# Two of the last weight loads of a mixture-of-experts layer, cut differently

## The chip, the cores and the metric

The kernel runs on one core of a Trainium2 chip. Its time is device time in microseconds (us), the median of three runs. The engines are TensorE (PE, with its weight loads as PEld), VectorE (DVE), ScalarE (ACT), GpSimd (POOL) and SyncE (SP). Nearly all loads from HBM are issued by SP; each transfer is carried by the core's 16 DMA engines, and each of them works through its own queue in the order in which the transfers were issued. A load has landed when the last of its DMA engines has reported.

## The reference

One decoder layer in float32 on 256 tokens of width 1024: attention and convolution branches, then 32 experts of which each token uses four, then a gated output with a layer norm. Cut to the part that matters here:

```python
for e in range(N_EXPERTS):                              # 32 experts
    gu = t @ w_gate_up[e] + b_gate_up[e]                # (1024 x 2048)
    g, u = gu[:, :D_EXPERT], gu[:, D_EXPERT:]
    g = jnp.minimum(g, SWIGLU_LIMIT); u = jnp.clip(u, -SWIGLU_LIMIT, SWIGLU_LIMIT)
    act = (u + 1) * (g * jax.nn.sigmoid(SWIGLU_ALPHA * g))
    y = act @ w_down[e] + b_down[e]                     # (1024 x 1024)
    out = out + combine[:, e:e + 1] * y
...
ple = jax.nn.sigmoid(h @ w_ple_gate) * (p @ w_ple_proj)
x = layer_norm(h + ple, ln2_g, ln2_b)
```

## The kernel before

The front of the layer takes the first 230 us. Then the experts run one after the other. For each, TensorE gathers the tokens that chose it, multiplies them with the gate and up weights, turns the sums, multiplies with the down weights and adds the rows to the output. An expert's weights are 12 MB in six pieces of 2 MB, c = 0 to 5: four of gate and up, two of down. Each piece is a tile of 128 partitions by 4096 floats (16 KB in a partition, `PAIR`) and feeds 16 records of matmuls of 128x512 (L488).

SP loads the pieces in the order in which TensorE uses them. They go into a ring of 11 places in SBUF (`slot_no`, `place_of`), and before each load SP waits until TensorE has read what lay there (`pair_read(last_in[n])`: `chunk_used`, `gu_done` or `d_done`). Pieces are numbered by `load_no(e, c)`. For the experts 5 to 29 two neighbouring pieces are joined to one transfer of 4 MB where their places lie side by side (the list `JOINED`); it waits for both places and raises one semaphore, for which both pieces wait on TensorE (`arrival`). Experts 30 and 31 are loaded in single pieces, and the last pieces of expert 31 in parts: piece 2 in its two rows (L401), piece 3 as its gate halves (L394) and then its two up halves (L396), piece 5 in two parts (L406). Behind them come two pieces of 2 MB of the gate of the output (L732, `w_pg`) and the two layer norm vectors (L735, L736). TensorE uses `w_pg` at L1398, in 128 records; the first 16 of these need the first piece alone.

Each semaphore `e_in[slot]` counts 16 for each transfer (`counts`), and TensorE waits in `pair(n)` for the count in `arrival[n]`. If an expert has more than 64 tokens it takes another branch with two rounds; in the run below the experts 29 to 31 take one round.

Of the kernel before, what the change touches and what calls it, by code (L numbers as in the profile page):

```python
# [7 lines left out]
D, S, P = 1024, 256, 128  # L8
# [9 lines left out]
NE, TOPE = 32, 4  # L18
# [24 lines left out]
PAIR = 2 * SLOT  # L43
# [39 lines left out]
def program(nc, x, xT, pT, w_in, consts1, consts2, b_in, w_oa, w_oc, w_out,  # L83
# [4 lines left out]
    with ctx:  # L88
# [3 lines left out]
        def sem(name):  # L92
            return ctx.enter_context(nc.semaphore(name))
# [5 lines left out]
        def view(at, n):  # L99
            return arena[:, at:at + n]  # L100
# [127 lines left out]
        e_in = [sem(f"expert_slot{i}_in") for i in range(ES)]  # L228
# [117 lines left out]
        PIECES = {6: 2, 10: 2, **{ES + i: 2 for i in range(CPE)}}  # L346
        slots, slot_no, last_in = list(range(ES)), [], []
# [7 lines left out]
        def place_of(n):  # L355

            return ((NF - NS + 1) // 2 % (NS // 2) + slot_no[n]) % ES

        def slot_of(n, size=PAIR):

            return view(RING + PAIR * place_of(n), size)

        def load_no(e, c):
            return e * CPE + c + (1 if e >= PP_E else 0)

        JOINED = [load_no(e, c) for e in range(5, NE - 2) for c in (0, 2, 4)]
        JOINED = [n for n in JOINED if place_of(n + 1) == place_of(n) + 1]
        counts, arrival = [0] * ES, []
        for n in range(NMP + CPE):
            if n == SPARE:  # L370
                arrival.append(None)
            elif n - 1 in JOINED:
                arrival.append(arrival[n - 1])
            else:
                counts[slot_no[n]] += 16 * PIECES.get(n, 1)
                arrival.append((slot_no[n], counts[slot_no[n]]))

        def rows_of_two(e, c):
            if c < 4:
                return w_gu[bass.ds(e, 1), c // 2 * 512:(c // 2 + 1) * 512, :].rearrange("e (p r) d -> p (e r d)", r=4)  # L380
            return w_dn[bass.ds(e, 1), :, :].rearrange("e p d -> p (e d)")

        def pair_source(e, c):
            return rows_of_two(e, c)[:, c % 2 * PAIR:(c % 2 + 1) * PAIR]

        def load_pair(sp, n, e, c, piece=None):
            if n == SPARE:
                for to, at in ((spare_row, slice(SLOT, PAIR)), (slot_of(n)[:, 0:SLOT], slice(0, SLOT))):
                    sp.dma_start(to, pair_source(e, c)[:, at]).then_inc(own_row_in, 16)
                return  # L390
            if n == LAST:
                to = slot_of(n).rearrange("p (r d) -> p r d", r=2)
                of = pair_source(e, c).rearrange("p (r d) -> p r d", r=2)
                sp.dma_start(to[:, :, 0:1024], of[:, :, 0:1024]).then_inc(e_in[slot_no[n]], 16)  # L394
                for r in range(2):
                    sp.dma_start(to[:, r, 1024:2048], of[:, r, 1024:2048]).then_inc(last_up_in[r], 16)  # L396
                return
            if n == LAST - 1:
                for row, done in enumerate((e_in[slot_no[n]], own_row_in)):
                    at = slice(row * SLOT, (row + 1) * SLOT)  # L400
                    sp.dma_start(slot_of(n)[:, at], pair_source(e, c)[:, at]).then_inc(done, 16)  # L401
                return
            if n == NG - 1:
                for half, done in enumerate((e_in[slot_no[n]], last_down_in)):
                    at = slice(half * SLOT, (half + 1) * SLOT)
                    sp.dma_start(slot_of(n)[:, at], pair_source(e, c)[:, at]).then_inc(done, 16)  # L406
                return
            if piece is not None:
                size = PAIR // PIECES[n]
                at = slice(piece * size, (piece + 1) * size)  # L410
                sp.dma_start(slot_of(n)[:, at], pair_source(e, c)[:, at]).then_inc(e_in[slot_no[n]], 16)
                return
            if n in JOINED:
                sp.dma_start(slot_of(n, 2 * PAIR), rows_of_two(e, c)).then_inc(e_in[slot_no[n]], 16)
                return
            sp.dma_start(slot_of(n), pair_source(e, c)).then_inc(e_in[slot_no[n]], 16)

        def pair_read(n):
            e, c = divmod(n - (1 if n > PP else 0), CPE)
            if c == 3:  # L420
                return gu_done, 2 * e + 2
            if c == CPE - 1:
                return d_done, 3 * e + 2
            return chunk_used, e * (CPE - 2) + (c + 1 if c < 4 else c)
# [228 lines left out]
        with nc.Block() as block:  # L653
            @block.sync
            def _(sp):
# [8 lines left out]
                def early(n, piece=None):  # L664
                    load_pair(sp, n, n // CPE, n % CPE, piece)
# [46 lines left out]
                for n in range(ES, NG):  # L712
                    if n in PIECES:
                        for i in range(PIECES[n] - 1):
                            sp.wait_ge(piece_used, pieces.up())
                            load_pair(sp, n, *divmod(n, CPE), i)
                        if n == ES + SPARE:
                            continue
                        sp.wait_ge(*pair_read(last_in[n]))
                        load_pair(sp, n, *divmod(n, CPE), PIECES[n] - 1)  # L720
                        continue
                    if n == PP or n - 1 in JOINED:
                        continue
                    sp.wait_ge(*pair_read(last_in[n]))
                    if n in JOINED:
                        sp.wait_ge(*pair_read(last_in[n + 1]))
                    load_pair(sp, n, *divmod(n - (1 if n > PP else 0), CPE))
# [1442 lines left out]
```

## Time and profile before

| | us |
|---|---|
| median of 3 runs | 1165.41 (1165.16 to 1165.5) |
| the profiled execution, its own time | 1165.17 |
| its span in the trace | 1163.3 |
| TensorE busy | 1134.7 (98% of the span) |
| 16 DMA engines, first queue (SP's loads) | 90.0% of 16 engines' span, 439.79 MB |

Read the busy shares with care: a TensorE that waits 2 us here and 1 us there for weights still counts as 98% busy. What a change to a late load is worth is read from the last wait for a DMA, and from how much later than its need each following load lands.

### The profile page before, as it was taken

To read this page: it belongs to the slowest core of one execution; us is meant where nothing else is said; L and a number is where in the kernel's file an instruction comes from. 1 tells how busy PE (TensorE), PEld (TensorE's weight loads), DVE (VectorE), ACT (ScalarE), POOL (GpSimd) and SP (SyncE) were. 2 spreads that over 40 slices of the span, in tenths; PEclk is the share of its full clock that TensorE was granted. 3 is DMA by queue.
4 is the path that set the end of the run, shared out by engine and by line. 5 is a ranking of instruction groups with operands and counts; after the bars stand their busy time and mean duration, and the time that the engine had idled before them with its cause. 6 is when DMAs were issued, how large, how long until landed. Compare 5 with 4: busy or idle time off the path is not lost.

```text
span 1163.3 us, 13812 instructions
## 1 busy us (share of the span) xinstructions
PE 1134.7 (98%) x5632; PEld 578.2 (50%) x5632; DVE 302.1 (26%) x790; ACT 182.5 (16%) x391; POOL 11.5 (1%) x26
## 2 busy tenths in 40 slices
PE   9999999999999999999999999999999999999997
PEld 7888888734344443434343344443434343433346
DVE  0549943411113122111111212121111111111126
ACT  1214220212121211111011011111111111101012
POOL 0020000000000000000000000000000000000000
PEclk9999999999999999999999999999999999999999
DMA  9975357699999999999999999999999999999981
GB/s 360 384 280 217 137 234 317 265 361 426 428 427 424 436 431 431 427 431 431 430 427 431 429 412 436 431 432 429 432 431 432 429 429 429 429 431 426 423 342 38
DMA packets 37564, 447.15 MB, mean 384 GB/s; under 512 B 3216, under 2 KB 6320, under 8 KB 19312
## 3 DMA queue, kind: packets, MB, share of 16 engines
q1 hardware_dynamic: 32896, 439.79, 90.0%
q10 hardware_dynamic: 4592, 6.33, 1.5%
q8 instruction: 50, 0.82, 0.3%
q14 instruction: 26, 0.21, 0.0%
HBM read 443.49 MB, written 2.62 MB: 383 GB/s over the span
## 4 chain that ended last, share of the span: by engine, by line
PE 81%; DMA 14%; DVE 3%; issue 1%; ACT 1%; SPq 0%; DVEq 0%; ACTq 0%
PE bank L488 49%; DMA arena<-in_w_gu 13%; PE bank L807 10%; PE bank L459 5%; PE bank L507 3%; PE bank L959 2%; PE bank L972 2%; PE bank L1398 2%; PE bank L494 2%; DMA arena<-in_w_in 1%; PE bank L841 1%; DVE arena L527 1%; PE bank L883 1%; DVE arena L547 0%; PE bank L482 0%
## 5 line engine op out<-in xcount | busy, mean ns | idle before, releaser
L488 PE MATMUL bank<-arena 128*64 128x512 f32 x3168 | 695.4, 595 | 14.3 <-DMA arena<-in_w_gu 9.8
L488 PEld LDWEIGHTS bank<-arena 128*64 128x64 f32 x3168 | 236.9, 137 | 435.8 <-issue 408.3
L527 DVE TENSOR_TENSOR arena<-bank,arena 128x512 f32<-128x512 f32 x32 | 22.1, 692 | 659.1 <-PE bank L494 659.1
L807 PE MATMUL bank<-arena 128*128 128x256 f32 x512 | 112.7, 380 | 0.0
L807 PEld LDWEIGHTS bank<-arena 128*128 128x128 f32 x512 | 96.7, 190 | 14.0 <-issue 1.3
L1563 ACT ACTIVATE arena<-bank 128x512 f32<-128x512 f32 x31 | 18.5, 597 | 361.3 <-PE bank L488 361.3
L507 PE MATMUL bank<-arena 64*128 64x512 f32 x272 | 67.9, 616 | 0.8 <-ACT arena L1570 0.7
L459 PEld LDWEIGHTS bank<-sel,arena 128*128 128x128 f32 x480 | 54.7, 192 | 11.4 <-issue 11.4
L459 PE MATMUL bank<-sel,arena 128*128 128x128 f32 x480 | 57.6, 279 | 0.0
L1570 ACT ACTIVATE arena<-bank 128x512 f32<-128x512 f32 x32 | 19.1, 597 | 214.9 <-PE bank L488 214.9
L1787 DVE SCALAR_TENSOR_TENSOR arena<-arena 128x256 f32<-128x256 f32 x120 | 48.5, 479 | 0.5 <-DVE arena L1787 0.2
L494 PEld LDWEIGHTS bank<-arena 128*128 128x128 f32 x264 | 27.3, 140 | 34.3 <-issue 31.7
L494 PE MATMUL bank<-arena 128*128 128x128 f32 x264 | 42.0, 284 | 0.2
L507 PEld LDWEIGHTS bank<-arena 64*128 64x128 f32 x272 | 23.4, 186 | 24.2 <-issue 22.5
L1460 ACT ACTIVATE arena<-bank,arena 128x256 f32<-128x256 f32 (+1 forms) x36 | 16.2, 466 | 90.3 <-PE bank L807 89.8
L972 PE MATMUL bank<-arena 128*128 128x256 f32 x128 | 28.5, 380 | 0.0
L547 DVE SCALAR_TENSOR_TENSOR arena<-arena 128x256 f32<-128x256 f32 x64 | 27.2, 425 | 4.2 <-DVE arena L543 0.4
L551 DVE TENSOR_TENSOR arena<-arena 128x256 f32<-128x256 f32 x64 | 27.2, 425 | 3.9
L959 PE MATMUL bank<-arena 128*128 128x256 f32 x128 | 27.9, 380 | 0.0
L1398 PE MATMUL bank<-arena 128*128 128x256 f32 x128 | 27.8, 379 | 0.0
L585 ACT ACTIVATE arena<-arena 128x512 f32<-128x512 f32 x33 | 20.8, 630 | 39.4 <-DVE arena L529 39.4
L533 DVE TENSOR_TENSOR arena<-bank,arena 128x256 f32<-128x256 f32 x64 | 26.7, 418 | 0.0
(223 smaller groups left out, 523.3 us busy)
## 6 DMA issues: line engine op xcount, KB each, us to landing
arena<-in_w_gu SPq DMA_DIRECT2D x47, 4096.0 KB, 31.7
arena<-in_w_dn SPq DMA_DIRECT2D x23, 4096.0 KB, 31.5
arena<-in_w_gu SPq DMA_DIRECT2D x26, 2048.0 KB, 14.3
arena<-in_w_dn SPq DMA_DIRECT2D x14, 2048.0 KB, 15.4
arena<-in_w_in SPq DMA_DIRECT2D x17, 1024.0 KB, 17.5
arena<-in_w_gu SPq DMA_DIRECT2D x15, 1024.0 KB, 8.4
arena<-in_w_dn SPq DMA_DIRECT2D x8, 1024.0 KB, 6.9
arena<-in_w_out SPq DMA_DIRECT2D x4, 1024.0 KB, 4.8
```

Of the source, the lines that this page charges most:

```text
L459: mm = pe.matmul(bank[b + k // 4][:, (k % 4) * P:(k % 4 + 1) * P], x1[:, t, k * P:(k + 1) * P], sel[:, t, :, :], start=(t == 0), stop=(t = ...
L488: mm = pe.matmul(to[half * CAP:(half + 1) * CAP, :], rows, w[:, half * 512:(half + 1) * 512], start=first, stop=last)
L494: mm = pe.transpose(to[:, j * P:(j + 1) * P], rows[:, j * P:(j + 1) * P], ident)
L507: mm = pe.matmul(total[t][n][:, :], G2[q][a:a + CAP, t * P:(t + 1) * P], rows[a:a + CAP, :], start=first, stop=last)
L527: nc.vector.tensor_tensor(by_bias(gt, 8), by_bias(of_gate[:, :], 8), bias_of(e, 0, 0, 8), ALU.add).then_inc(sw_step, 1)
L547: nc.vector.scalar_tensor_tensor(up[:, at], up[:, at], 1.0, gt[:, at], ALU.add, ALU.mult).then_inc(sw_step, 1 + 6 * skip * j)
L551: nc.vector.tensor_tensor(to[:, at], up[:, at], sg[:, at], ALU.mult).then_inc(act_ready, 1 + 2 * skip * j)
L807: mm = pe.matmul(bank[n % 4][:, lo:S], w[:, k, j * P:(j + 1) * P], xT_sb[:, k, lo:S], start=(k == 0), stop=(k == KD - 1))
L959: mm = pe.matmul(bank[n % 4][:, 0:S], w_view(i)[:, k, (c % 4) * P:(c % 4 + 1) * P], rhs[:, k, :], start=(k == 0), stop=(k == 3))
L972: mm = pe.matmul(mix_bank(t, j), merged[:, k, t * P:(t + 1) * P], w_view(25 + j)[:, k, :], start=(k == 0), stop=(k == KD - 1))
L1398: mm = pe.matmul(gate_bank(t, j), hT[:, k, t * P:(t + 1) * P], pg_view(k, j), start=(k == 0), stop=(k == KD - 1))
L1787: nc.vector.scalar_tensor_tensor(cy[:, a, :], u_sb[:, a, bass.ds(j, S)], dw[:, a, bass.ds(j, 1)], cy[:, a, :], ALU.mult, ALU.add).then_inc ...
```

## The change

The list `JOINED` loses the number `load_no(29, 2)`: pieces 2 and 3 of expert 29, one transfer of 4 MB before, become two transfers of 2 MB with a wait and a semaphore each. And piece 0 of expert 30 (`EVENED`), one transfer of 128 rows before, becomes ten: of 80, 36, 5 and then seven times one row. A row is one partition with 16 KB. By the words of the change this gives the first DMA engine 16 rows and the last four 5 each, where each had 8; 80 rows are 5 for each of 16, 36 are 3 for each of 12, 5 are 1 for each of 5, and the seven single rows all go to the first. So the engines 1 to 4 get 9, and 5 to 11 keep 8. The semaphore of that place then counts 160 in place of 16.

```diff
-        JOINED = [n for n in JOINED if place_of(n + 1) == place_of(n) + 1]
+        JOINED = [n for n in JOINED if place_of(n + 1) == place_of(n) + 1 and n != load_no(NE - 3, 2)]
+        EVENED = load_no(NE - 2, 0)
+        GROUPS = [(0, 80), (80, 36), (116, 5)] + [(p, 1) for p in range(121, P)]
...
-                counts[slot_no[n]] += 16 * PIECES.get(n, 1)
+                counts[slot_no[n]] += 16 * (len(GROUPS) if n == EVENED else PIECES.get(n, 1))
...
+            if n == EVENED:
+                to, of = slot_of(n), w_gu[e, c // 2 * 512:(c // 2 + 1) * 512, :].rearrange("(p r) d -> p (r d)", r=4)
+                for p0, size in GROUPS:
+                    sp.dma_start(to[p0:p0 + size, :], of[p0:p0 + size, c % 2 * PAIR:(c % 2 + 1) * PAIR]
+                                 ).then_inc(e_in[slot_no[n]], 16)
+                return
```

On SP, from the gate and up pieces 0 and 1 of expert 29 (first row) to piece 1 of expert 31, before:

```order
126 L414 DMA arena<-in_w_gu 128x8192 [waits gu_done,chunk_used]
127 L414 DMA arena<-in_w_gu 128x8192 [waits d_done,chunk_used]
128 L414 DMA arena<-in_w_dn 128x8192 [waits chunk_used]
129 L416 DMA arena<-in_w_gu 128x4096 [waits chunk_used]
130 L416 DMA arena<-in_w_gu 128x4096 [waits gu_done]
131 L416 DMA arena<-in_w_gu 128x4096 [waits chunk_used]
132 L416 DMA arena<-in_w_gu 128x4096 [waits d_done]
133 L416 DMA arena<-in_w_dn 128x4096 [waits chunk_used] x2
134 L416 DMA arena<-in_w_gu 128x4096 [waits chunk_used]
135 L416 DMA arena<-in_w_gu 128x4096 [waits gu_done]
```

The same stretch of SP now:

```order
126 L422 DMA arena<-in_w_gu 128x8192 [waits gu_done,chunk_used]
127 L424 DMA arena<-in_w_gu 128x4096 [waits chunk_used]
128 L424 DMA arena<-in_w_gu 128x4096 [waits d_done]
129 L422 DMA arena<-in_w_dn 128x8192 [waits chunk_used]
130 L408 DMA arena<-in_w_gu 80x4096 [waits chunk_used]
131 L408 DMA arena<-in_w_gu 36x4096
132 L408 DMA arena<-in_w_gu 5x4096
133 L408 DMA arena<-in_w_gu 1x4096 x7
134 L424 DMA arena<-in_w_gu 128x4096 [waits gu_done]
135 L424 DMA arena<-in_w_gu 128x4096 [waits chunk_used]
136 L424 DMA arena<-in_w_gu 128x4096 [waits d_done]
137 L424 DMA arena<-in_w_dn 128x4096 [waits chunk_used] x2
```

The joined load has become two, of which the first no longer waits for `d_done`; the load behind the down pieces of expert 29 has become ten; nothing else on SP has moved.

On TensorE, the gate and up matmuls of expert 29 (pieces 0 and 1 wait for the semaphore of slot 2), before:

```order
1034 L488 MATMUL bank<-arena 64x512 [waits expert_slot2_in]
1035 L488 MATMUL bank<-arena 64x512 x7
1036 L488 MATMUL bank<-arena 64x512 [waits expert_slot2_in]
1037 L488 MATMUL bank<-arena 64x512 x7
1038 L488 MATMUL bank<-arena 64x512 [waits expert_slot4_in]
1039 L488 MATMUL bank<-arena 64x512 x7
1040 L488 MATMUL bank<-arena 64x512 [waits expert_slot4_in]
1041 L488 MATMUL bank<-arena 64x512 x7
```

And now:

```order
1036 L496 MATMUL bank<-arena 64x512 [waits expert_slot2_in]
1037 L496 MATMUL bank<-arena 64x512 x7
1038 L496 MATMUL bank<-arena 64x512 [waits expert_slot4_in]
1039 L496 MATMUL bank<-arena 64x512 x7
1040 L496 MATMUL bank<-arena 64x512 [waits expert_slot5_in]
1041 L496 MATMUL bank<-arena 64x512 x7
```

No instruction of TensorE has moved. Piece 3 now waits for a semaphore of its own (slot 5), so the matmuls of piece 2 wait for the first transfer alone.

## Rows read from the trace of the kernel before

**Rows 1.** The page: busy time, speed of the DMAs in 40 slices, the final chain

```profile
PE 1134.7 (98%) x5632; PEld 578.2 (50%) x5632; DVE 302.1 (26%) x790; ACT 182.5 (16%) x391; POOL 11.5 (1%) x26
...
GB/s 360 384 280 217 137 234 317 265 361 426 428 427 424 436 431 431 427 431 431 430 427 431 429 412 436 431 432 429 432 431 432 429 429 429 429 431 426 423 342 38
...
PE 81%; DMA 14%; DVE 3%; issue 1%; ACT 1%; SPq 0%; DVEq 0%; ACTq 0%
```

**Rows 2.** Waits of TensorE: us in total, times, longest; whole span

```profile
PE bank L488 <- DMA arena<-in_w_gu: 9.8, 8, 2.6
```

**Rows 3.** The chain in order of time, from 880 us: start, us, what

```profile
1013.48 37.17 DMA arena<-in_w_gu
...
1050.69 8.51 PE bank L488 x32
```

**Rows 4.** TensorE in order of time: start, us, instructions [idle before, releaser]

```profile
1040.97 7.09 PE L488 MATMUL bank<-arena 128*64 128x512 f32 x32 [1.60 <-DMA arena<-in_w_gu]
1050.69 8.51 PE L488 MATMUL bank<-arena 128*64 128x512 f32 x32 [2.63 <-DMA arena<-in_w_gu]
...
1073.41 13.96 PE L488 MATMUL bank<-arena 128*64 128x512 f32 x64
...
1091.01 19.96 PE L488 MATMUL bank<-arena 128*64 128x512 f32 x92 [0.16 <-DVE arena L551]
...
1115.73 7.09 PE L488 MATMUL bank<-arena 128*64 128x512 f32 x32 [0.46 <-DVE arena L580]
...
1127.75 3.62 PE L1398 MATMUL bank<-arena 128*128 128x256 f32 x16
```

**Rows 5.** Stretches: us, busy by engine, granted clock, DMA share, GB/s

```profile
1050.00:1053.60 3.60, 2.91 (x8) 0.99 (x10) 0.00 (x0) 0.00 (x0) 0.00 (x0) 0.53 0.99 428
1060.00:1090.00 30.00, 30.00 (x158) 12.93 (x156) 5.67 (x15) 4.58 (x9) 0.00 (x0) 1.00 1.01 427
```

**Rows 6.** SP in order of time: start, us of issuing, loads

```profile
1025.24 14.49 SPq L416 DMA_DIRECT2D arena<-in_w_gu  x4
...
1055.81 3.76 SPq L416 DMA_DIRECT2D arena<-in_w_gu  x2
...
1073.15 0.38 SPq L394 DMA_DIRECT2D arena<-in_w_gu  x1
1073.57 9.41 SPq L396 DMA_DIRECT2D arena<-in_w_gu  x2
1083.03 4.24 SPq L416 DMA_DIRECT2D arena<-in_w_dn  x1
...
1096.49 5.65 SPq L732 DMA_DIRECT2D arena<-in_w_pg  x2
```

**Rows 7.** Landings (last figure: us from issue), of the issues at 1025.2, 1028.7, 1039.4

```profile
arena<-in_w_gu SPq DMA_DIRECT2D x1, 2048.0 KB, 40.0
...
arena<-in_w_gu SPq DMA_DIRECT2D x1, 2048.0 KB, 41.5
...
arena<-in_w_gu SPq DMA_DIRECT2D x1, 2048.0 KB, 40.5
```

**Rows 8.** Landings of the issues at 1055.8, 1059.2, 1073.2, 1083.0; both of L732

```profile
arena<-in_w_gu SPq DMA_DIRECT2D x1, 2048.0 KB, 38.8
...
arena<-in_w_gu SPq DMA_DIRECT2D x1, 2048.0 KB, 40.3
...
arena<-in_w_gu SPq DMA_DIRECT2D x1, 1024.0 KB, 33.9
...
arena<-in_w_dn SPq DMA_DIRECT2D x1, 2048.0 KB, 31.5
...
DMA to landing us min/median/max: 27.9/30.8/33.8
```

**Rows 9.** DMA share (last but one) after the last `w_pg` packets begin to run out

```profile
1123.00:1124.00 1.00, 0.44 (x2) 0.30 (x4) 0.00 (x0) 0.51 (x1) 0.00 (x0) 1.00 0.93 389
1125.00:1126.00 1.00, 1.00 (x8) 0.42 (x4) 1.00 (x3) 0.00 (x0) 0.00 (x0) 1.00 0.84 348
1127.00:1128.00 1.00, 1.00 (x9) 0.80 (x8) 0.20 (x1) 0.99 (x3) 0.00 (x0) 1.00 0.62 250
1130.00:1131.00 1.00, 1.00 (x7) 0.87 (x6) 0.00 (x0) 0.00 (x0) 0.00 (x0) 1.00 0.31 127
```

**Rows 10.** Instruction packets in the queues, 1118 to 1131 us: packets, MB, share of 16 engines

```profile
q8 instruction: 1, 0.02, 0.5%
```

## The prediction

> **What bounds the kernel now.** I read five views, in this order. The page shows a TensorE that is 98% busy and DMAs that move 412 to 436 GB/s in all slices from 260 us to about 1105 us, while 14% of the chain that ended last is DMA [rows 1]: both are close to their limit, and the end is set by whichever is later, piece by piece. The list of waits shows only 9.8 us of waiting of TensorE for gate and up weights, in 8 waits, the longest 2.6 us [rows 2]. The chain says where the last of them lies: a load issued at 1013.48 runs 37.17 us, lands at 1050.65, and from 1050.69 to the end nothing but TensorE, with short steps of the other engines, stands in it [rows 3]. So a gain before 1050.65 would be lost in this wait, and a gain behind it counts until another load comes late. The timeline shows the wait's size: the 32 records of pieces 0 and 1 of expert 29 run from 1040.97 to 1048.06, those of pieces 2 and 3 start at 1050.69 after 2.63 us of idle time, and take 8.51 us where 32 such records take 7.09 [rows 4]. The stretches say why: the granted clock from 1050.0 to 1053.6 is 0.53, which is nearly all time at the lower level of 1.2 GHz, and 1.00 from 1060 to 1090 [rows 5]. The fall follows the idle 2.63 us; the wait of 1.60 us before the row at 1040.97 was followed by 7.09 us, without a loss [rows 4].
>
> **The joined load in two.** Consecutive single pieces land 4.9 us apart: the issue at 1025.24 lands 40.0 us later at 1065.2, the next one, 3.43 us behind it (four issues in 14.49 us with their waits; the second is at 1028.67), 41.5 us later at 1070.2 [rows 6, 7]. The order within each DMA engine does not change, so the first 2 MB of the old load land 4.9 us before 1050.65, at 1045.8, and the second at 1050.65. SP issues the first no later than now, since its wait for `d_done` is gone. TensorE is free at 1048.06, finds piece 2, and needs piece 3 16 records (3.5 us) later, at 1051.6: it is there. The wait of 2.63 us goes, and with it the reason for the slow clock, 8.51 - 7.09 = 1.42 us. Together **4.05 us**. Bounds: 2.63, if the clock falls all the same, to 4.05. One more transfer costs the DMA queues little: 4.2 MB at the 431 GB/s of the slices with joined loads take 9.7 us, at the 427 of the stretch with single ones 9.8 [rows 1, 5], so 0.1 us at most.
>
> **What is late next.** Here most of the 4.05 us is lost. For each later load I take when TensorE needs it now, less when it lands; 16 records are 3.5 us. Piece 3 of expert 30: needed 48 records after 1073.41, at 1083.8; issued at 1039.40, landed 40.5 later at 1079.9: 3.9 us to spare [rows 4, 6, 7]. Piece 0 of expert 31: needed at 1091.01 plus 32 records, 1098.0; issued 1055.81, landed 1094.6: 3.4. Piece 1: needed 1101.4, issued 1059.24, landed 1099.5: 1.9. The gate halves of piece 3: needed 80 records after 1091.01, at 1108.4; issued 1073.15, landed 1107.05: 1.3. The first down piece of expert 31: needed 1115.73, issued 1083.03, landed 1114.5: **1.2**. The second piece of `w_pg`: TensorE starts L1398 at 1127.75 and needs it 16 records later, at 1131.2; the second issue starts near 1097.0 and lands 33.8 us later, at 1130.8: **0.4** [rows 4, 6, 8]. These spares are not added: each says by how much TensorE can be early there, and the smallest behind a point is what is left of the gain. The parts of pieces 2, 3 and 5 that I leave out have 1.5 us or more. So the split alone would give 0.4 us, set by `w_pg`; with that load out of the way 1.2.
>
> **The uneven load.** It moves all landings behind it by the same amount as it moves the latest DMA engine. A row is 4.9 / 8 = 0.61 us of one engine. Four engines do 3 rows less: 1.8 us earlier for good. Engines 1 to 4 do 1 more: 0.6 us. The first does 8 more: 4.9 us. Is there such a spread? The profile has no view by DMA engine, but the end shows it: no piece follows the second of `w_pg`, and the DMA share falls to 0.84 by 1125 to 1126, to 0.62 two us later, and is 0.31 at 1130 to 1131, when that piece lands [rows 9]. Some engines are thus done 5 us before the last. A cause stands in the queues: one packet of instructions, 16 KB, whose 0.5% of 16 engines over 13 us are 1.0 us of a single engine [rows 10], and that piece lands 6.4 us behind the first one (1124.4 to 1130.8) where 4.9 is the rule [rows 6, 8]. So one fetch puts about 1.5 us on one engine, and engines that get them fall behind. Bounds of what the uneven load gives to landings: for the second piece of `w_pg`, 0 if its latest engine is none of the last four, 1.5 to 1.8 if it is; for the others, from 1.8 earlier (if only these four are late) down to about 0, since such fetches fall on several engines and the next latest then decides. I take 1.5 for `w_pg` and 0.1 for the rest net of the split's cost: only four of 16 are relieved, and the first engine, with 4.9 us more against a lead of about 5, may be the next one itself. Then the down piece leaves 1.2 + 0.1 = **1.3 us**, `w_pg` 1.9, and 1.3 is what reaches the end, where only TensorE and the tail behind it follow.
>
> **The issues.** Ten transfers take SP ten times 0.33 us, with what lies between perhaps 4 us, from 1025.2 on; the issue at 1028.67 moves by less than 1 us. The queue in front of it is 40 us deep [rows 7], and that hides it. Later SP is held up by full queues already: L396 takes 9.41 us for two issues, L416 then 4.24 for one [rows 6]. More entries in the first engine's queue may make that begin earlier, but a full queue is no idle engine. If this cover were gone, each 1 us would cost 1 us of landing; the DMA share of 1.01 from 1060 to 1090 speaks against it [rows 5].
>
> **A rule that speaks against it.** The diff's single rows have one partition and 4096 elements. The Trainium skill, page "DMA: Bandwidth & Descriptors", section "Why a DMA increments its semaphore by 16 and not by 1", says that a transfer uses the largest number up to 16 of engines that divides the slowest dimension whose size isn't 1, and the lowest-numbered ones. By that 80, 36 and 5 rows go as the change says, but a single row has only the 4096 elements left to divide, and would be spread over all 16. No transfer of the trace tells, since all have 32 rows or more.
>
> **Rivals.** (a) *The latest engine of `w_pg` is not relieved*: its spare stays 0.4, gain 0.3 to 0.5, 1164.9 to 1165.1. For it: twelve of 16 engines are not relieved. Against: the last four would hardly be spared without being late. (b) *The relief goes deep*: the last four are the only late ones, all landings come 0.9 to 1.8 us earlier, the down piece then leaves 2.1 to 3.0 us: 1162.4 to 1163.3. Against: 16 KB fetches would have to fall on few engines. (c) *Slower: the first engine becomes the latest.* If its lead over the latest is only 0 to 1.9 us in place of 5, all later landings come 3.0 to 4.9 us later, the down piece makes TensorE 1.8 to 3.7 us late: 1167.2 to 1169.1. It turns to a loss where the lead is under 4.9 - 1.2 = 3.7 us. For it: it gets more extra work than any lead that I can read with certainty. (d) *The change doesn't do what it says*: single rows are cut over all 16 engines, so each gets 7/16 row more, 0.3 us, and the first 9.4 rows and no more. The last four still gain 1.5 us. The down piece leaves 1.2 - 0.3 = 0.9, or up to 1.2 where the latest engine is one of the last four: 1164.2 to 1164.5. Its pieces are a sixteenth of 16 KB for each engine, of which the trace has no row.
>
> **The numbers.** The profiled execution took 1165.17, of which 1163.3 is span; 1.3 us less is 1163.9. The median is 0.24 above that execution, so I predict **1164.1**. A measurement of this kernel can tell a change from none from about 0.2% (2.3 us): faster is below 1163.1, slower above 1167.7. Chances: my forecast (gain 0.9 to 1.7) 0.50, (a) 0.17, (b) 0.13, (c) 0.12, (d) 0.08. Faster gets most of (b), 0.10; slower most of (c), 0.09; the rest, 0.81, is within. The range leaves out half of (b) and most of (c): 1162.9 to 1166.4; its upper part also holds a first engine that is late by a little.
>
> **What would show it.** After 1048 no wait for a DMA of 2.6 us and a clock of 1.00 from 1050 to 1054; the matmuls of piece 2 of expert 29 start near 1048.1, and expert 30 begins some 4 us earlier, near 1069.4. Then two or three waits of TensorE that are not there now: some 0.5 us at piece 0 of expert 31, 1.4 at piece 1, 0.5 at the gate halves of piece 3, so that the last down matmuls start near 1114.4. The second piece of `w_pg` should land near 1129.3. If it lands at 1130.8 with a wait in L1398, (a) holds; if all landings from 1065 on are 3 us later, (c); if they are 1 us earlier, (b). The step that I trust least is the 0.1 us for the ordinary landings; the prediction fails outright if the first DMA engine had no lead.

## The result: 1% slower

The kernel after takes 1176.78 us in the median of four runs (1175.42 to 1180.3), the kernel before 1165.45 beside it: a ratio of 1.0101 with a 95% interval of 1.0089 to 1.0114, so 11.3 us slower, where 1164.1 and at most 1166.4 were predicted. The profiled execution is the slowest of the four, 1180.3 us with a span of 1178.6, and so shows 15.3 us more span than that of before.

### The profile page after: what moved, and what is told of

It reads as the page before. It is cut to its first block, busy times and chain, and to the rows that moved or that the text cites. A ratio compares the mean times of both kernels' runs of the same rounds, so it can differ in the third digit from the quotient of the medians.

```text
span 1178.6 us, 13821 instructions
## 1 busy us (share of the span) xinstructions
PE 1135.9 (96%) x5632; PEld 576.7 (49%) x5632; DVE 301.9 (26%) x790; ACT 182.5 (15%) x391; POOL 11.5 (1%) x26
## 3 DMA queue, kind: packets, MB, share of 16 engines
q1 hardware_dynamic: 33064, 439.79, 90.1%
## 4 chain that ended last, share of the span: by engine, by line
PE 79%; DMA 15%; DVE 3%; issue 2%; SPq 1%; ACT 0%; DVEq 0%; ACTq 0%
PE bank L496 48%; DMA arena<-in_w_gu 14%; PE bank L815 9%; PE bank L467 4%; PE bank L515 3%; PE bank L967 2%; PE bank L980 2%; PE bank L1406 2%; PE bank L502 2%; DMA arena<-in_w_in 1%; PE bank L849 1%; DVE arena L535 1%; PE bank L891 1%; PE bank L490 1%; DVE arena L555 0%
## 5 line engine op out<-in xcount | busy, mean ns | idle before, releaser
L496 PE MATMUL bank<-arena 128*64 128x512 f32 x3168 | 696.5, 595 | 27.7 <-DMA arena<-in_w_gu 15.1
L496 PEld LDWEIGHTS bank<-arena 128*64 128x64 f32 x3168 | 235.8, 137 | 451.6 <-issue 412.8
L1406 PE MATMUL bank<-arena 128*128 128x256 f32 x128 | 27.8, 379 | 0.0
```

The source lines that it names most:

```text
L496: mm = pe.matmul(to[half * CAP:(half + 1) * CAP, :], rows, w[:, half * 512:(half + 1) * 512], start=first, stop=last)
L1406: mm = pe.matmul(gate_bank(t, j), hT[:, k, t * P:(t + 1) * P], pg_view(k, j), start=(k == 0), stop=(k == KD - 1))
```

## The profile after

All line numbers behind the edit are 8 higher than before (L488 is now L496, L1398 is L1406); the loop of the ten transfers is L408.

From the page: the granted clock and the speed of the DMAs in 40 slices of 29.5 us, SP's queue and the final chain, to be read beside [rows 1]:

```profile
PEclk9999999999999999999999999999999999998999
...
GB/s 360 383 267 217 155 238 283 302 370 424 436 411 434 428 433 428 433 428 433 424 435 428 427 431 429 432 430 429 429 434 428 431 430 435 428 370 264 422 338 37
...
q1 hardware_dynamic: 33064, 439.79, 90.1%
...
PE 79%; DMA 15%; DVE 3%; issue 2%; SPq 1%; ACT 0%; DVEq 0%; ACTq 0%
```

The speed falls to 370 and 264 GB/s in two slices near the end of the experts, where the kernel before has 431 and 426 in the slices with the same numbers [rows 1]. The 168 packets more in SP's queue (33064 against 32896) are 128 of the load that was split (32 KB in a partition before, twice 16 KB now) and 40 short ones, one for each DMA engine that takes part in a transfer: 16 for the second half of the split load, and for the ten transfers 16 + 12 + 5 + 7 = 40 in place of 16. The semaphore of the changed piece agrees: DMA engines raise it 40 times in the trace. So a single row goes to one engine, as one packet. No view names the engine.

TensorE in order of time (start, us, instructions, in brackets the idle time before and what ended it), which answers to [rows 4]:

```profile
1041.29 13.95 PE L496 MATMUL bank<-arena 128*64 128x512 f32 x64 [1.62 <-DMA arena<-in_w_gu]
...
1070.33 8.80 PE L496 MATMUL bank<-arena 128*64 128x512 f32 x32 [8.20 <-issue]
...
1081.83 3.65 PE L496 MATMUL bank<-arena 128*64 128x512 f32 x16 [2.33 <-DMA arena<-in_w_gu]
1086.48 3.65 PE L496 MATMUL bank<-arena 128*64 128x512 f32 x16 [1.00 <-DMA arena<-in_w_gu]
1091.38 3.65 PE L496 MATMUL bank<-arena 128*64 128x512 f32 x16 [1.24 <-DMA arena<-in_w_gu]
1096.27 3.65 PE L496 MATMUL bank<-arena 128*64 128x512 f32 x16 [1.24 <-DMA arena<-in_w_gu]
...
1110.95 3.65 PE L496 MATMUL bank<-arena 128*64 128x512 f32 x16 [0.30 <-DMA arena<-in_w_gu]
1115.87 7.09 PE L496 MATMUL bank<-arena 128*64 128x512 f32 x32 [1.27 <-DMA arena<-in_w_gu]
1123.38 2.80 PE L496 MATMUL bank<-arena 128*64 128x512 f32 x12 [0.43 <-DMA arena<-in_w_gu]
...
1130.94 7.09 PE L496 MATMUL bank<-arena 128*64 128x512 f32 x32 [0.45 <-DVE arena L588]
```

The first row is what the prediction wanted: pieces 0 to 3 of expert 29 in one run, without the wait of 2.63 us and without the slow matmuls at 1050.69. What comes next was not in it. The down matmuls of expert 29 start after 8.20 us of idle time and take 8.80 us where 7.09 is the rule, and behind them seven groups of gate and up matmuls find their weights late. The name "issue" means that the profile shows no releaser, but the load tells it. The joined load of these down pieces, in the DMA view of its issue at 1021.16 (last figure: us from issue to landing):

```profile
arena<-in_w_dn SPq DMA_DIRECT2D x1, 4096.0 KB, 49.1
```

It lands at 1070.26, and 0.07 us later the matmuls start. Behind the changed piece, the load issued at 1028.97 in the same view:

```profile
arena<-in_w_gu SPq DMA_DIRECT2D x1, 2048.0 KB, 57.5
```

It took 41.5 us before [rows 7], so 16.0 us less. The waits of TensorE for these weights (us in total, times, longest), which answer to [rows 2], are 13.5 us more than before in sum:

```profile
PE bank L496 <- DMA arena<-in_w_gu: 15.1, 13, 2.3
PE bank L496 <- issue: 8.2, 1, 8.2
```

The stretches show the reason (us; busy time of PE, PEld, DVE, ACT and POOL; then granted clock, DMA share, GB/s), to be read beside [rows 5]:

```profile
1045.00:1050.00 5.00, 5.00 (x26) 1.66 (x24) 0.00 (x0) 0.00 (x0) 0.00 (x0) 1.00 1.00 426
1050.00:1055.00 5.00, 5.00 (x26) 1.51 (x22) 0.00 (x0) 0.60 (x1) 0.00 (x0) 1.00 1.16 374
1055.00:1060.00 5.00, 5.00 (x33) 3.22 (x32) 3.65 (x9) 1.29 (x3) 0.00 (x0) 1.00 1.05 206
1060.00:1065.00 5.00, 2.13 (x20) 1.94 (x18) 0.42 (x1) 1.19 (x2) 0.00 (x0) 1.00 0.92 190
1065.00:1070.00 5.00, 0.00 (x0) 0.00 (x0) 0.00 (x0) 0.00 (x0) 0.00 (x0) 0.70 1.00 165
1070.00:1075.00 5.00, 4.67 (x14) 1.62 (x16) 0.00 (x0) 0.00 (x0) 0.00 (x0) 0.62 0.98 141
1075.00:1080.00 5.00, 4.50 (x22) 1.45 (x18) 0.00 (x0) 0.77 (x2) 0.00 (x0) 1.00 0.95 236
1080.00:1085.00 5.00, 3.17 (x16) 1.06 (x16) 0.00 (x0) 0.10 (x1) 0.00 (x0) 1.00 1.00 406
```

From 1055 to 1080 the DMA engines are as busy as ever, 0.92 to 1.05 by their share, and move 141 to 236 GB/s, about half or less; the fall begins near 1052. A share near 1.0 with half the bytes means that the packets themselves take longer. In the packets of the trace, which no view lists, the medians are 0.61 us for 16 KB and 1.22 for 32 KB before 1052, and 1.25 and 2.43 from 1060 to 1065. The packets of 32 KB there belong to the joined down load of 128 rows that was issued ahead of the ten transfers: so the ten transfers, once some engines had come to them, slowed down engines that were still in the load before.

The later groups pay as follows. The last down matmuls start at 1130.94, and in the run with the split alone (below) at 1115.06, so 15.9 us apart: 0.5 from the start at 1041.29 against 1040.81, 8.20 for the stall, 8.80 - 7.09 = 1.71 for the clock (0.70 and 0.62 after the idle time), 4.93 for the waits that follow (2.33, 1.00, 1.24, 1.24, 0.30, 1.27 and 0.43 here, against 0.88, 0.30, 1.25 and 0.45 there), and 0.43 because 64 matmuls run in four groups in place of two. That is 15.8.

## The theories

The forecast's own gain could be there and be outweighed, or be missing. And the loss could lie in four things: the first engine's 16 rows, many small transfers or single rows, where a transfer's rows lie in HBM, or the partitions that the transfers write. Letters of theories in the expectations are those of the expectation in which they are explained. Each run below is timed beside the kernel before, on the same chip, and its ratio is to that; the medians of the kernel before are 1165.99 us for runs 1 to 4, 1165.77 for 5 to 8, 1166.12 for 9 and 10, and 1166.04 for 11 and 12. The edits are those against the kernel after; all change only how piece 0 of expert 30 is loaded, but for the second.

## Run 1: the split alone

```diff
-        GROUPS = [(0, 80), (80, 36), (116, 5)] + [(p, 1) for p in range(121, P)]
+        GROUPS = [(0, P)]
```

> The joined load in two, piece 0 of expert 30 as one transfer of 128 rows again. Theory A (the uneven load alone does the harm, whatever its form): packets keep 0.61 us for 16 KB, the wait of 2.63 us and the slow clock behind it go, and the second piece of w_pg leaves 0.4 us of gain: 0.2 to 0.6 us under the kernel before, about 1165.0. Theory B (the split itself does the harm, for instance through fuller queues): several us slower than before.

Measured: 1165.2 us against 1165.99, ratio 0.9994 (0.9985 to 1.0003, 11 runs). TensorE in order of time:

```profile
1040.81 13.95 PE L496 MATMUL bank<-arena 128*64 128x512 f32 x64 [1.61 <-DMA arena<-in_w_gu]
...
1068.97 10.52 PE L496 MATMUL bank<-arena 128*64 128x512 f32 x48
1080.37 3.65 PE L496 MATMUL bank<-arena 128*64 128x512 f32 x16 [0.88 <-DMA arena<-in_w_gu]
...
1095.06 3.65 PE L496 MATMUL bank<-arena 128*64 128x512 f32 x16 [0.30 <-DMA arena<-in_w_gu]
1099.96 7.09 PE L496 MATMUL bank<-arena 128*64 128x512 f32 x32 [1.25 <-DMA arena<-in_w_gu]
1107.50 2.80 PE L496 MATMUL bank<-arena 128*64 128x512 f32 x12 [0.45 <-DMA arena<-in_w_gu]
...
1115.06 7.09 PE L496 MATMUL bank<-arena 128*64 128x512 f32 x32 [0.46 <-DVE arena L588]
...
1127.08 27.79 PE L1406 MATMUL bank<-arena 128*128 128x256 f32 x128
```

This is the timeline that the prediction drew. Expert 30 starts at 1068.97 (1069.4 was forecast), 4.44 us earlier than before [rows 4], and the waits behind it take nearly all of that back. The prediction said waits of 0.5, 1.4 and 0.5 us at the pieces 0 and 1 of expert 31 and its gate halves, and they are 0.30, 1.25 and 0.45. Piece 3 of expert 30 was said to have 3.9 us to spare against a start 4.05 us earlier, so a wait of 0.15; it is 0.88. The last down matmuls start 0.67 us earlier than before, and the span is 0.6 us shorter. Neither is more than the measurement can tell from nothing. The joined down load, issued at 1020.71:

```profile
arena<-in_w_dn SPq DMA_DIRECT2D x1, 4096.0 KB, 40.0
```

So the 49.1 us of the kernel after come from the ten transfers behind it, not from the split. The stretch in which the kernel after moves 165 GB/s:

```profile
1065.00:1070.00 5.00, 5.00 (x26) 1.67 (x24) 0.00 (x0) 0.87 (x2) 0.00 (x0) 1.00 1.00 423
```

## Run 2: the uneven load alone

```diff
-        JOINED = [n for n in JOINED if place_of(n + 1) == place_of(n) + 1 and n != load_no(NE - 3, 2)]
+        JOINED = [n for n in JOINED if place_of(n + 1) == place_of(n) + 1]
```

> The ten transfers alone, with the load of expert 29 joined as before. Theory A: the same stretch of about 27 us with DMA rates near half, so 11 to 15 us slower than before, as in the changed kernel, and the wait of 2.63 us is there as well. Theory B: no more than 1 us away from before.

Measured: 1178.46 us, ratio 1.0099 (1.0084 to 1.0115). TensorE, with the old wait of the joined load and the new one behind it:

```profile
1051.87 7.09 PE L496 MATMUL bank<-arena 128*64 128x512 f32 x32 [2.64 <-DMA arena<-in_w_gu]
...
1067.81 8.77 PE L496 MATMUL bank<-arena 128*64 128x512 f32 x32 [1.96 <-issue]
```

This is 12.5 us more than the kernel before beside it, as theory A says: the whole loss comes from the ten transfers. The wait before 1067.81 is only 1.96 us, because TensorE comes to it 3.72 us later than in the kernel after (1065.85 against 1062.13): the old wait of 2.64 us is taken from the new one, and so the split saves nothing here either.

## Runs 3 and 4: two even transfers

```diff
-        GROUPS = [(0, 80), (80, 36), (116, 5)] + [(p, 1) for p in range(121, P)]
+        GROUPS = [(0, 80), (80, 48)]
```

> Split as in the change, and piece 0 of expert 30 in two transfers of 80 and 48 rows: 5 and 3 rows for each of the 16 DMA engines, so every engine has 8 rows as in one transfer and none is in only a part of it. Theory A1 (rows that are cut other than 128 at a time put several engines on the same part of SBUF, and they wait for each other): the rate halves for the time of this load, a loss of 3 to 8 us against the split alone. Theory A2 (the harm is in the first engine's 16 rows and the transfers with fewer than 16 engines): packets keep 0.61 us, and the time is that of the split alone within 0.3 us.

Measured: 1177.47 us, ratio 1.0097 (1.0082 to 1.0113). One of its slow stretches:

```profile
1060.00:1065.00 5.00, 2.76 (x25) 2.57 (x23) 0.89 (x3) 1.19 (x2) 0.00 (x0) 1.00 0.92 193
```

```diff
-        GROUPS = [(0, 80), (80, 36), (116, 5)] + [(p, 1) for p in range(121, P)]
+        GROUPS = [(0, 64), (64, 64)]
```

> Split as in the change, and piece 0 of expert 30 in two transfers of 64 rows, the lower and the upper half of the partitions: 4 and 4 rows for each engine. Theory A1: as slow as 80 and 48 rows or slower, since all 16 engines write into one half of the partitions at a time. Theory A2: the time of the split alone within 0.3 us.

Measured: 1174.63 us, ratio 1.0078 (1.0063 to 1.0094). Its stretches:

```profile
1055.00:1060.00 5.00, 5.00 (x35) 3.40 (x34) 4.08 (x10) 1.19 (x4) 0.00 (x0) 1.00 1.02 233
1060.00:1065.00 5.00, 2.02 (x17) 1.70 (x17) 0.00 (x0) 1.01 (x2) 0.00 (x0) 0.96 1.01 226
1065.00:1070.00 5.00, 5.00 (x18) 1.74 (x16) 0.00 (x0) 0.00 (x0) 0.00 (x0) 0.70 1.00 215
```

In both, each of the 16 engines gets eight rows, as in an ordinary load, and there is no single row and no first engine with 16. The loss is 11 and 9 us: A1 has the right kind of cause, but its 3 to 8 us for run 3 were too few. So neither the first engine's 16 rows nor single rows are the main cause. With the halves the speed is 215 to 233 GB/s, half of 430.

## Runs 5 to 7: which side it is

Two transfers of 64 rows, once every second partition written from 64 neighbouring rows, once 64 neighbouring partitions written from every second row, and once every second row to every second partition. In the first two the rows of this piece stand in another order than the matmuls need, so part of expert 30's sum is another one; nothing is left out.

```diff
+        HALVES = [slice(0, 64), slice(64, 128)]
+        EVEN_ODD = [slice(0, 127, 2), slice(1, 128, 2)]
+        GROUPS = [0, 1]
...
-                for p0, size in GROUPS:
-                    sp.dma_start(to[p0:p0 + size, :], of[p0:p0 + size, c % 2 * PAIR:(c % 2 + 1) * PAIR]
+                for h in GROUPS:
+                    sp.dma_start(to[EVEN_ODD[h], :], of[HALVES[h], c % 2 * PAIR:(c % 2 + 1) * PAIR]
```

> As the 64 and 64 rows (split kept), but each transfer writes every second partition (all of SBUF's width) from the same contiguous halves of the rows in HBM; the rows of this one piece come out in another order, so the result of expert 30 is not the reference's. Theory S (the halves are slow because all engines write into one half of SBUF's partitions): the rate stays near 427 GB/s, or falls for less long than with halves, and most of the 9 us is back. Theory H (reading the halves from HBM is what is slow): as slow as 64 and 64, about 1174.6.

Measured: 1165.22 us, ratio 0.9995 (0.9985 to 1.0006):

```profile
1060.00:1065.00 5.00, 5.00 (x37) 3.50 (x37) 1.05 (x3) 1.19 (x2) 0.00 (x0) 1.00 1.01 429
1065.00:1070.00 5.00, 5.00 (x25) 1.57 (x22) 0.00 (x0) 0.00 (x0) 0.00 (x0) 1.00 1.03 431
```

For the second, `to[HALVES[h], :]` and `of[EVEN_ODD[h], ...]`:

> The reverse: each transfer writes one half of the partitions, lower then upper, from every second row in HBM; again the rows of this one piece are in another order. Theory S: as slow as 64 and 64, near 1174.6, with 215 to 233 GB/s for some 19 us. Theory H: about the time of the split alone, 1165.2.

Measured, in two executions: 1176.42 us, ratio 1.0091 (1.0071 to 1.0111):

```profile
1060.00:1065.00 5.00, 3.74 (x32) 3.55 (x32) 1.83 (x5) 1.19 (x2) 0.00 (x0) 1.00 0.91 203
1065.00:1070.00 5.00, 2.53 (x12) 1.09 (x14) 0.00 (x0) 0.00 (x0) 0.00 (x0) 1.00 1.02 228
```

For the third, `EVEN_ODD[h]` on both sides:

> Two transfers of 64 rows that take every second row from HBM into every second partition, so the result is the reference's. Theory S: like the run that writes every second partition. Theory H: between; if both sides had to be contiguous over 128 rows it is as slow as 64 and 64. If any transfer other than 128 rows is slow, whichever partitions it writes, then this one and the first of this call are as slow as 64 and 64.

Measured: 1164.87 us, ratio 0.9995 (0.9984 to 1.0007), 418 to 436 GB/s in all stretches from 1050 on.

The place in HBM isn't it: reading every second row costs nothing in run 7 and does not help in run 6. (Run 6 is 1.8 us above the 1174.6 that theory S named, which two executions can't tell from run 4.) The speed hangs on the partitions that a transfer writes. Two transfers of 64 rows that each reach over the whole width are free, two that take a half each cost 9 to 11 us.

## Runs 8 to 10: how much of the width

```diff
-        GROUPS = [(0, 80), (80, 36), (116, 5)] + [(p, 1) for p in range(121, P)]
+        GROUPS = [(0, 112), (112, 16)]
```

> Two transfers of 112 and 16 rows, 7 and 1 for each engine, split kept. Theory S: 112 rows reach nearly all of SBUF's width and only the 16 rows are crowded, so the rate is low for a few us alone and the loss is well under that of 64 and 64: 1 to 5 us against the split alone. If any transfer other than 128 rows is slow: 9 us or more.

Measured: 1175.8 us, ratio 1.0082 (1.0065 to 1.0099), where 1 to 5 us were expected:

```profile
1055.00:1060.00 5.00, 5.00 (x35) 3.58 (x35) 4.07 (x10) 1.20 (x3) 0.00 (x0) 1.00 1.03 226
1060.00:1065.00 5.00, 1.35 (x13) 1.16 (x11) 0.00 (x0) 0.80 (x2) 0.00 (x0) 1.00 0.95 180
```

With `GROUPS = [(0, 120), (120, 8)]`:

> Split kept; piece 0 of expert 30 in transfers of 120 rows (the first 15 engines with 8 rows each) and 8 rows (the first 8 engines with one). Theory M (each DMA engine writes the 8 neighbouring partitions that it also has in a transfer of 128 rows, and what slows all is one engine writing where another one does): 120 rows are then as free as 128, only the 8 rows written by engines 0 to 7 into the place of engine 15 are crowded, and the low rate lasts 5 us or less: a loss of 1 to 4 us against the split alone. Theory N (any transfer that doesn't span all 128 partitions is slow as long as others run beside it): near half rate from the first of the 120 rows on, a loss of 8 to 12 us as with 112 and 16.

Measured: 1175.05 us, ratio 1.0082 (1.0065 to 1.01):

```profile
1060.00:1065.00 5.00, 3.24 (x30) 3.05 (x28) 1.33 (x4) 1.19 (x2) 0.00 (x0) 1.00 0.96 223
1065.00:1070.00 5.00, 3.49 (x10) 1.18 (x12) 0.00 (x0) 0.00 (x0) 0.00 (x0) 0.54 0.96 221
1070.00:1075.00 5.00, 5.00 (x22) 1.76 (x20) 0.00 (x0) 0.00 (x0) 0.00 (x0) 0.78 0.99 220
```

And with 120 rows and eight single ones, `GROUPS = [(0, 120)] + [(p, 1) for p in range(120, P)]`:

> The same 120 rows, and then eight transfers of one row, all on the first engine: it gets 16 rows, engines 1 to 14 get 8, engine 15 none. It has the changed kernel's load on the first engine without its 80, 36 and 5 rows. Theory M: the first engine's 8 rows take 4.9 us more and all go into the place of engine 15, which is then at half speed; the others run on, so the loss is 1 to 5 us. Theory P (single rows on one engine are the main harm of the change): 8 us or more, with the low rate during the single rows. Theory N: 10 us or more, with the low rate from the 120 rows on.

Measured: 1174.84 us, ratio 1.0077 (1.006 to 1.0094).

The idea behind the first two expectations, that the cost grows with the part of the width that is missing, fell: 120 of 128 rows cost as much as a half. Nor do eight single rows on the first engine cost more than one transfer of eight. This left two theories. C: what counts is which engine writes which partitions. By it, in an ordinary load each engine writes a group of partitions of its own, and another split sends several engines into the same group at once. N: any transfer that does not reach over the whole width slows everything beside it.

## Runs 11 and 12: eight rows apart and eight together

Both load only partitions 0 to 63 of the piece, in eight transfers of eight rows, each row a packet of 16 KB for one of eight engines. Only the places of the eight rows differ.

```diff
-        GROUPS = [(0, 80), (80, 36), (116, 5)] + [(p, 1) for p in range(121, P)]
+        GROUPS = [slice(h + a, h + a + 29, 4) for h in (0, 32) for a in range(4)]
...
-                for p0, size in GROUPS:
-                    sp.dma_start(to[p0:p0 + size, :], of[p0:p0 + size, c % 2 * PAIR:(c % 2 + 1) * PAIR]
+                for rows in GROUPS:
+                    sp.dma_start(to[rows, :], of[rows, c % 2 * PAIR:(c % 2 + 1) * PAIR]
```

> Split kept. Of piece 0 of expert 30 only partitions 0 to 63 are loaded, the other 64 rows are left out; they come in eight transfers of eight rows, and in each the rows stand 4 partitions apart (0, 4, ... 28; then 1, 5, ... 29; and so on, then the same from 32). Each of these transfers can occupy eight DMA engines with one row each, so eight engines get eight rows as in an ordinary load, and eight get none and go ahead. Theory C (collision): in a transfer over 128 partitions each DMA engine writes a set of partitions of its own, four here and four 32 further; the halved rates came from transfers in which several engines write into one such set at a time. Here the eight engines of a transfer write eight different sets: the rate stays at 380 to 430 GB/s from 1050 to 1080 us, no wait of TensorE above 2 us for this, median 1163.5 to 1166.5. Theory N (any transfer that doesn't reach over all 128 partitions halves the rate of everything beside it): rates of 200 to 250 GB/s for 10 us or more, median 1170 to 1178, as in the runs with 64, 80, 112 or 120 rows.

Measured: 1164.5 us against 1166.04, ratio 0.9986 (0.9977 to 0.9996):

```profile
1055.00:1060.00 5.00, 5.00 (x35) 3.48 (x34) 4.07 (x10) 1.20 (x3) 0.00 (x0) 1.00 0.95 406
1060.00:1065.00 5.00, 5.00 (x31) 2.60 (x32) 0.00 (x0) 0.89 (x2) 0.00 (x0) 1.00 1.00 421
1065.00:1070.00 5.00, 5.00 (x26) 1.55 (x24) 0.00 (x0) 0.87 (x2) 0.00 (x0) 1.00 1.02 429
```

And the same with `GROUPS = [slice(a, a + 8) for a in range(0, 64, 8)]`:

> The same as the run with eight rows apart, with the same 64 rows in eight transfers of eight rows, the rest left out, but the eight rows of a transfer stand side by side (0 to 7, 8 to 15, ...). The same number of packets of 16 KB for the same DMA engines; only which partitions the eight engines write at a time differs. Theory C: eight engines write into two sets at a time, four into each, so such a row takes up to four times 0.61 us, the eight transfers 19.6 us in place of 4.9, and the engines behind them are held up: later landings up to 15 us late, total rate halved or worse for 10 to 20 us, median 1172 to 1182. Theory N: the same loss as with the rows apart, within 2 us.

Measured: 1170.98 us, ratio 1.0047 (1.003 to 1.0064):

```profile
1055.00:1060.00 5.00, 5.00 (x36) 3.77 (x36) 3.54 (x10) 1.23 (x2) 0.00 (x0) 1.00 0.94 213
1060.00:1065.00 5.00, 1.54 (x9) 0.87 (x9) 0.00 (x0) 0.60 (x1) 0.00 (x0) 0.87 1.00 252
1065.00:1070.00 5.00, 5.00 (x22) 1.78 (x20) 0.00 (x0) 0.00 (x0) 0.00 (x0) 0.79 0.97 247
1070.00:1075.00 5.00, 5.00 (x26) 1.70 (x24) 0.00 (x0) 0.87 (x2) 0.00 (x0) 1.00 0.98 387
```

Transfers of eight rows, none of which reaches over more than 29 partitions, keep 406 to 429 GB/s when the rows stand 4 apart; N falls. As many packets of the same size, in as many transfers, into eight neighbouring partitions bring 213 to 252 GB/s for 15 us. (The rows in HBM differ with them, but runs 5 to 7 show that their place does not matter.) So with eight rows to a transfer the partitions alone decide: neighbouring ones cost, rows 4 apart do not. That the cost comes from several engines writing into the same group at once is what C adds; it fits, also with the load of 128 rows being free, but no view shows which engine writes which partition. Two things of C's expectation were off. The median is 1 us under the 1172 that was its lower end. And the estimate of 19.6 us for the eight transfers is more than the 15 us of slow stretches; perhaps the engines with no row of this piece were slowed less, but no view shows an engine by itself. The 1.5 us by which run 11 lies below the kernel before is no gain to keep: half of a piece isn't loaded there, and the interval overlaps that of run 1.

The Trainium skill has a map that fits this. Its page "SBUF — State Buffer", section "Door 1: The DMA port swizzle (why [64,N] ≈ [32,N])", says that 16 ports take the DMAs' writes, each for two groups of four partitions that are 32 apart, and that partitions 0 to 63 reach eight of them, for about 218 GB/s. Run 4 agrees with 215 to 233 GB/s. By the same map the eight rows of run 11 go to eight ports and those of run 12 to two, which agrees with both. The same page, section "Can I just issue two DMAs to hit both halves?", says that the only way to reach all 16 ports is one transfer over all 128 partitions; the 406 to 429 GB/s of run 11, with transfers of eight rows, speak against that as a rule of speed while other loads run beside. The Trainium skill's page "DMA: Bandwidth & Descriptors", section "The descriptor swizzle", gives each engine of an ordinary load one port of its own. An estimate from the two pages: if 120 rows are instead dealt out in order, eight to an engine, then engines 0 to 3 and 4 to 7 write the same ports at a time and the speed would be half, about 215 of 430; the 220 to 223 GB/s of run 9 agree. No run shows the port of a packet.

## Why the prediction was wrong, point by point

**Bounds now and the split: right.** The wait of 2.63 us and the slow matmuls behind it went, as forecast, and without the uneven load the spares of the later loads left about what the prediction said. It gave 0.4 or 1.2 us for the split alone, and run 1 shows 0.6 of span. Only the wait for piece 3 of expert 30 is 0.7 us longer than worked out.

**The second `w_pg` piece: not the limit.** It was given 0.4 us to spare. In run 1 no wait stands in L1406, and the piece lands at 1129.6, 28.8 us after its issue at 1100.8, where TensorE needs it 16 records after 1127.08, at 1130.7: 1.1 us to spare.

```profile
DMA to landing us min/median/max: 28.8/30.5/32.3
```

**The uneven load: the step that failed.** The prediction said "It moves all landings behind it by the same amount as it moves the latest DMA engine" and priced a row at 4.9 / 8 = 0.61 us of one engine, whatever transfer it comes in. That price is the one of a row in a transfer of 128, and it was carried over to shapes that the trace did not have. Here no packet of 16 KB took less than 1.15 us from 1055 to 1075, the median of each 5 us was 1.25 to 1.77, and engines that were still in the load ahead were slowed as well. The step took bounds of 0 to 1.8 us earlier, and what came was landings 9.5 us later for the load ahead (1070.26 against 1060.75 in run 1) and 16 us for one behind it. What stands in its place: a load cut into blocks of neighbouring partitions holds the speed of all transfers together near half, also with eight rows for each engine (runs 3 and 4). The sentence "No transfer of the trace tells, since all have 32 rows or more" was used against one rule only; the same lack of rows should have opened the price of every new shape upwards, which is what the bounds had to do.

**The rule on single rows.** By the words of the Trainium skill, page "DMA: Bandwidth & Descriptors", section "Why a DMA increments its semaphore by 16 and not by 1", a row would be spread over 16 engines. The trace of after has one packet of 16 KB and one short packet for each single row, so rival (d) is out, and the numbers of engines are those that the change says; which engines they are, no view shows.

**Rival (c)** had the right sign and the wrong mechanism. It put the loss at 3.0 to 4.9 us per landing on the first engine alone. Runs 3 and 4, in which the first engine has its eight rows, lose 11 and 9 us; run 10, in which it has 16, loses 9. So the 0.09 for slower was not a forecast of this cause, and the first engine's lead, which the prediction called its weak point, was not what decided.

**The issues: right.** Ten transfers took SP 3.18 us at L408, the next issue stands at 1028.97 where it was 1028.67.

**The slow clock came back in another place.** The prediction tied it to idle time in which TensorE waits. It is so again: 1.71 us after the stall of 8.20, with a granted clock of 0.70 and 0.62 in those stretches, so partly at the lower level of 1.2 GHz.

**The check it named.** It said that landings 3 us later from 1065 on would mean (c). They were 10 to 16 us later. And the DMA share, which it had read as a sign that the engines keep up (1.01 from 1060 to 1090), stayed near 1.0 in the kernel after while the speed halved.

**What stays open.** Why 64 rows at every second partition are free when they too, dealt out in order, would put several engines into one group: if C is the reason, some other order of dealing must hold there, and no run shows it. Why 80 + 48 rows cost 11 us, as much as the change itself, and 64 + 64 or 120 + 8 only 9, isn't settled (the intervals of runs 3 and 4 overlap); the first engine's 16 rows show no cost of their own that these runs could tell. Whether an uneven load without such collisions would gain anything was not tried. No version was found that beats the kernel before by more than the measurement can tell: the best with all of its work, runs 1 and 7, are at 0.9994 and 0.9995.

## What to carry to other kernels

A transfer's price is not its bytes by the rate of its neighbours: it hangs on which partitions it writes together, and one load of 2 MB cut into blocks of rows held the speed of all transfers near half for 15 to 27 us here. So in a stretch that is bound by DMAs, leave the transfers at 128 rows and cut them along the free dimension; if the rows must be cut, take them apart and not in blocks. What was free here is 64 rows at every second partition and eight rows at every fourth. And read GB/s beside the DMA share, since the share stays at 1.0 while the speed halves.

## What the runs showed of the hardware that was not expected

- Two loads of 64 neighbouring partitions, 112 + 16 and 120 + 8 all give about the same: 180 to 239 GB/s in the stretches of 5 us that are slow from end to end, in place of 410 to 433, and 9 to 11 us.
- The slowdown reaches the other DMA engines and transfers. The last and the first engine are 7.5 us apart in a landing of run 1 (the sixteen increments of the semaphore of piece 0 of expert 30 stand between 1058.17 and 1065.65), and pieces land 4.9 us apart, so a transfer meets parts of two or three others. In the kernel after, packets of the load of 128 rows ahead took 2.4 us in place of 1.22.
- A transfer has one short packet for each engine that takes part. By these counts 36 rows occupy 12 engines, five rows five, and a single row one, as one packet of 16 KB (16 + 12 + 5 + 7 = 40 in the kernel after). Eight rows occupy eight, as 120 + 8 rows (run 9) have 7 short packets more than the one load of 128 of run 1, which is 15 + 8 in place of 16, and the eight transfers of runs 11 and 12 have 48 more.
- Rows 4 partitions apart in transfers of eight cost nothing beside full loads (run 11: 406 to 429 GB/s); eight neighbouring rows bring about half the speed (run 12: 213 to 252).
